# Attention sweep: the order of transposes, scores and value products on TensorE, and of evictions and sigmoids on ScalarE

## What is computed

```python
for nb in range(seq // 128):                      # blocks of 128 queries
    z = einsum('bhtd,bhsd->bhts', qh[t0:t1], kh[:t1]) * scale
    mask = s < t
    log_keep = where(mask, log_sigmoid(-z), 0)
    rc = cumsum(log_keep, axis=keys, reverse=True)
    after = concatenate([rc[..., 1:], 0])
    w = where(mask, exp(log_sigmoid(z) + after), 0)
    out = einsum('bhts,bhsd->bhtd', w, vh[:t1])
```

## Time and profile before

| | us |
|---|---|
| median of 3 runs | 3290.05 |
| lowest and highest | 3288.12, 3293.3 |
| the profiled execution | 3288.1 |
| its span, first to last instruction | 3286.3 |

### The profile page before, as it was taken

How to read it: one execution, slowest core, us unless ns; L and a number is a source line. 1 busy time by engine, 2 the same in 40 slices (tenths; PEclk the granted TensorE clock), 3 DMA queues, 4 the chain that set the end, 5 groups by cost and what they waited for, 6 DMA issues and landing times. The chain is left out here.

```text
span 3286.3 us, 56906 instructions
## 1 busy us (share of the span) xinstructions
PE 3110.6 (95%) x22432; PEld 2724.4 (83%) x22432; DVE 1502.1 (46%) x1651; ACT 975.2 (30%) x1749; POOL 496.8 (15%) x218
## 2 busy tenths in 40 slices
PE   7899999999999999998888859999999999979998
PEld 6788888888999999998888857777777777768887
DVE  4212221111112311122888848778767877654433
ACT  4211111111111111110110126766666767631111
POOL 3211111111011101110664521000000000000000
PEclk8999999999999999999999989999999999989999
DMA  7113444443122221222444336523552351053221
GB/s 277 58 61 97 122 121 121 121 121 115 60 71 70 70 74 58 70 70 111 138 139 145 103 89 144 129 53 78 129 124 58 78 129 40 14 180 121 80 99 38
DMA packets 217944, 327.14 MB, mean 100 GB/s; under 512 B 11680, under 2 KB 159520, under 8 KB 204960
## 3 DMA queue, kind: packets, MB, share of 16 engines
q1 hardware_dynamic: 217296, 324.08, 33.0%
q10 hardware_dynamic: 464, 0.63, 0.1%
HBM read 207.22 MB, written 117.44 MB: 99 GB/s over the span
## 5 line engine op out<-in xcount | busy, mean ns | idle before, releaser
L1092 DVE TENSOR_TENSOR_SCAN run<-akeep 128x768 f32<-128x768 f32 (+7 forms) x256 | 425.5, 1698 | 172.2 <-ACT akeep L1056 122.3
L1064 ACT ACTIVATE wt<-t_ps 128x512 f32<-128x512 f32 (+3 forms) x640 | 314.1, 536 | 129.7 <-PE t_ps L985 128.7
L1056 ACT ACTIVATE akeep<-z_ps 128x1024 f32<-128x1024 f32 (+7 forms) x384 | 291.1, 778 | 155.6 <-PE z_ps L974 144.0
L1006 PE MATMUL o_ps<-wt,ad 128*64 128x128 f32 x4352 | 308.1, 280 | 5.5 <-issue 5.5
L985 PE MATMUL t_ps<-ident,run 128*128 128x128 f32 x2176 | 311.8, 278 | 0.1
L969 PE MATMUL z_ps<-ak,aq 128*128 128x512 f32 (+3 forms) x640 | 253.5, 396 | 40.2 <-DMA aq<-s_qlo 33.7
L370 PE MATMUL u_ps<-w_hi,h_lo 128*128 128x256 f32 x2048 | 287.5, 283 | 0.0
L370 PE MATMUL u_ps<-w_hi,h_hi 128*128 128x256 f32 x2048 | 287.5, 283 | 0.0
L370 PE MATMUL u_ps<-w_lo,h_hi 128*128 128x256 f32 x2048 | 287.5, 283 | 0.0
L1006 PEld LDWEIGHTS o_ps<-wt,ad 128*64 128x64 f32 x4352 | 231.2, 136 | 58.7 <-issue 57.9
L985 PEld LDWEIGHTS t_ps<-ident,run 128*128 128x128 f32 x2176 | 242.3, 141 | 45.1 <-issue 18.7
(11 more groups left out here) (140 smaller groups left out, 3837.7 us busy)
## 6 DMA issues: line engine op xcount, KB each, us to landing
w_raw<-in_w_in SPq DMA_DIRECT2D x32, 1024.0 KB, 5.7
aq<-s_qhi SPq DMA_DIRECT2D x64, 256.0 KB, 6.4
aq<-s_qlo SPq DMA_DIRECT2D x64, 256.0 KB, 7.0
o<-s_o SPq DMA_DIRECT2D x16, 1024.0 KB, 6.3
ada<-in_w_ada SPq DMA_DIRECT2D x9, 1024.0 KB, 7.5
xg<-in_x SPq DMA_DIRECT2D x4, 2048.0 KB, 10.7
s_gq<-st SPq DMA_DIRECT2D x32, 256.0 KB
s_gf<-st SPq DMA_DIRECT2D x32, 256.0 KB
```

Source lines behind the costliest of these rows:

```text
L1006: mm = nc.tensor.matmul(o_ps[e * SD:(e + 1) * SD, cols], delta[:, b, key // P + j, e * SD:(e + 1) * SD], wt[:, a % 8, j * P:(j + 1) * P], ...
L1056: nc.scalar.activation(keepf[:, e, n % 2, 0:width], z_ps[e][:, 0:width], ACT.Sigmoid, scale=-SCALE).then_inc(keep_ready, 1)
L1064: nc.scalar.activation(wt[:, a % 8, 0:wd], t_ps[a % 2][:, 0:wd], ACT.Identity, scale=-1.0, bias=1.0).then_inc(wt_ready, 1)
L1092: nc.vector.tensor_tensor_scan(run[:, e, qb % 2, at0:at0 + width][:, ::-1], keepf[:, e, n % 2, 0:width][:, ::-1], keepf[:, e, n % 2, 0:width],
```

## The change

Nothing is computed differently. The order in a step changes on two engines:
- TensorE: transposes of A (piece n - 2), scores of A and of B (piece n), transposes of B (piece n - 2), then all value products of piece n - 3 in one row. `weighted` loses its chunk argument and waits once, for the eviction of B's last chunk.
- ScalarE: the evictions of A, both sigmoids, the evictions of B.

```diff
-                def weighted(i, n, c):
+                def weighted(i, n):
...
-                    pe.wait_ge(wt_ready, i * (4 * NS) + (lists[1][c][0] + 1))
-                    key, wd = lists[0][c][1:]
-                    for j in range(wd // P):
-                        for e in range(2):
...
+                    pe.wait_ge(wt_ready, i * (4 * NS) + (last_part(n, 1) + 1))
+                    for c in range(len(lists[0])):
+                        key, wd = lists[0][c][1:]
+                        for j in range(wd // P):
+                            for e in range(2):
...
                 def step(i, n, last):
-                    for e in range(2):
-                        if there(n, last):
-                            scores(i, n, e)
-                    for e in range(2):
-                        if there(n - LAG_T, last):
-                            transposes(i, n - LAG_T, e)
-                        if there(n - LAG_AV, last):
-                            weighted(i, n - LAG_AV, e)
+                    if there(n - LAG_T, last):
+                        transposes(i, n - LAG_T, 0)
+                    if there(n, last):
+                        scores(i, n, 0)
+                        scores(i, n, 1)
+                    if there(n - LAG_T, last):
+                        transposes(i, n - LAG_T, 1)
+                    if there(n - LAG_AV, last):
+                        weighted(i, n - LAG_AV)
...
+                    n1 = n - LAG_T
+
+                    def evict(e):
+                        for a, key, wd in part_list(n1, e):
+
+                            act.wait_ge(t_ready, i * (4 * NS) + (a + 1))
+                            nc.scalar.activation(wt[:, a % 8, 0:wd], t_ps[a % 2][:, 0:wd], ACT.Identity, scale=-1.0,
+                                                 bias=1.0).then_inc(wt_ready, 1)
+
+                    if there(n1, last):
+                        evict(0)
                     if there(n, last):
...
-                    n1 = n - LAG_T
                     if there(n1, last):
-                        for e in range(2):
-                            for a, key, wd in part_list(n1, e):
...
+                        evict(1)
```

More of the change, by code:

```diff
@@ L992, in weighted @@
                     lists = [part_list(n, e) for e in range(2)]
-                    if c >= len(lists[0]):
-                        return
-                    if c == 0 and diag and qb % 4 == 0:
+                    if diag and qb % 4 == 0:
                         pe.wait_ge(ot_ready, i * 8 + (4 * (n // NP) + qb // 4 + 1))
-                    if c == 0 and n % NP == 0:
+                    if n % NP == 0:
                         pe.wait_ge(delta_ready, i * 2 + (n // NP + 1))
                     cols = slice((qb % 4) * P, (qb % 4 + 1) * P)
-                    pe.wait_ge(wt_ready, i * (4 * NS) + (lists[1][c][0] + 1))
-                    key, wd = lists[0][c][1:]
-                    for j in range(wd // P):
-                        for e in range(2):
[L1005 to L1010, removed]
+                    pe.wait_ge(wt_ready, i * (4 * NS) + (last_part(n, 1) + 1))
[3 more added lines that the diff above has]
+                            for e in range(2):
+                                a = lists[e][c][0]
+                                mm = nc.tensor.matmul(o_ps[e * SD:(e + 1) * SD, cols], delta[:, b, key // P + j, e * SD:(e + 1) * SD],
+                                                      wt[:, a % 8, j * P:(j + 1) * P], start=(diag and key == lo and j == 0),
+                                                      stop=(lo == 0 and key + (j + 1) * P == width))
+                    mm.then_inc(av_ready, 1)
                 def rows(i, n):
@@ L1057, in step @@
                                                  scale=-SCALE).then_inc(keep_ready, 1)
-                    n1 = n - LAG_T
                     if there(n1, last):
-                        for e in range(2):
-                            for a, key, wd in part_list(n1, e):
-                                act.wait_ge(t_ready, i * (4 * NS) + (a + 1))
-                                nc.scalar.activation(wt[:, a % 8, 0:wd], t_ps[a % 2][:, 0:wd], ACT.Identity, scale=-1.0,
-                                                     bias=1.0).then_inc(wt_ready, 1)
+                        evict(1)
                 sweep(nc.scalar, step)
```

## The result

The changed kernel takes 3241.42 us (median, 3241.3 to 3247.25) against 3289.09 us for the kernel before. The ratio is 0.9859, 95% interval 0.9842 to 0.9876: 1.4% faster. Two more comparisons gave 0.9869 (0.9854 to 0.9884) and 0.9863 (0.9847 to 0.9880), with medians of 3246.39 against 3290.1 and 3242.65 against 3287.79. So the change saves 44 to 48 us where 38.4 were forecast. The direction and the mechanism hold, the size was too small.

The account below looks back on a forecast made before the run. The prediction took TensorE's own row of work as the bound; 42.7 us saved by fewer switches, less 1.3 and 3 of waits, gave 38.4 us, so about 3251.5 us, range 3244 to 3268.

Parts of the forecast that it names:

- The bound: Attention sweep: TensorE is the bound, busy 196.8 of 200 us; only shortening its own row of work can help.
- The price of a change of work: Sweep steps whose value products have two chunks: fewer switches save 0.34 us in 112 steps, 0.29 in 16, together 42.7.
- The 0.29 for the steps with row transposes: In 16 two-chunk steps, row transposes stand between value products and scores; saving taken as 0.29 us each.
- T(A) before narrow scores: Transposes of A ahead of a narrow diagonal score block: 0 to 0.02 us, at most 32 times, taken as 0.
- The tail, 1.3 us: Last three steps: two waits of 0.4 us for A's eviction and 0.5 for the final value products, 1.3 us lost.
- The 0.5 for the last value products: End of the sweep: the final value products wait for B's last eviction, 0.5 us lost.
- ScalarE's margin: Steps with wide scores and one-chunk value products: B's eviction finishes 0.1 to 0.2 us in time, cost taken as 0.
- VectorE's cover at piece 12: Transposes of piece 12 wait 0.6 us for a scan delayed by GpSimd's subtraction, in six pairs; taken as 3 us.
- Sum: Whole kernel: 42.7 - 1.3 - 3 = 38.4 us saved, giving 3249.7 us profiled and a median of about 3251.5.
- The rival of scans met too early in more pieces: Transposes of A also wait for scans in two or three pieces a pair, about 15 us more: 3266; chance 0.17.
- The slower rival: Late scans hold transposes, scores and the next scan; 1.2 us waits in pieces 10 to 15, 3306 us; chance 0.05.
- The rival that no gain is there: TensorE's drain is paid wherever other data starts, or in-order waits replace it: 3290 us; chance 0.06.

Follow-up runs that it names:

- The cut runs: Changed kernel with value products split again: chunk 0 before the transposes of B, chunk 1 behind them; 3304.93 us, ratio 1.0044 to the kernel before.
- run 128*128: Not a follow-up run: in the profile rows of the transposes, the buffer `run` that they read, with its 128*128 shape; no time or ratio of its own.
- the block gone: Changed kernel with GpSimd subtracting only a sixteenth of each values block for the last six pairs of heads; 3243.08 us, ratio 0.9856.
- the block doubled: Changed kernel with GpSimd subtracting each values block twice, one after the other; 3278.78 us, ratio 0.9972.

## Why the prediction was right or wrong

- *The bound.* Right. TensorE's own row, without waits, set the sweep's time, and it does so again after the change.
- *The price of a change of work, 0.34 us for each two-chunk step.* Right in sum. 5.47 us for a pair of heads without a loop turn (109.83 to 104.36 in the traces) over 16 steps is 0.342. The 0.29 for the steps with row transposes was slightly low: 5.34 forecast for a pair, 5.47 measured, 1 us in all. The cut runs settled that the run is what costs, at 0.30 each; the other 0.04 come with the order.
- *T(A) before narrow scores: taken as 0.* Right within 0.06 us: T to Z is 0.03 in the order of starts for widths of 128 and 256, 0.08 for 384.
- *The tail, 1.3 us.* A little too large. The two waits of T(B) for A's eviction came, as 0.34 us of idle engine each; by the starts T(B) follows after 1.43 us instead of 0.87, so each cost 0.56 (0.4 forecast). The 0.5 for the last value products did not come: they stand behind those of the piece before, 64 instructions in a row, and the first 32 give 1.7 us of cover. 1.1 us in all.

```profile
2821.32 1.09 PE L985 MATMUL t_ps<-ident,run 128*128 128x128 f32 x8
2822.75 1.07 PE L985 MATMUL t_ps<-ident,run 128*128 128x128 f32 x8 [0.34 <-ACT wt L1055]
2823.75 3.71 PE L1005 MATMUL o_ps<-wt,ad 128*64 128x128 f32 x64
```

- *ScalarE's margin, taken as 0 cost.* Right. No transposes wait for an eviction in the steady state; the two waits in the waits' view are those of the tail.
- *VectorE's cover at piece 12, taken as 3 us of wait.* This is the term that failed. The new order took what was forecast: in the eighth pair, where no block is near, the cover went from 6.57 us to 3.39, 3.2 less (2.2 + 0.65 + 0.34). The block was to lie 1.7 us later against TensorE and leave the transposes 0.6 us short. The store and the load are as I had them (2637.20 to 2657.24, 20.0 us), and against the start of scan A the subtraction began 1.6 us later (1.42 us ahead of it, 3.04 before). But it took 4.56 us and not 5.53. Before, it had begun at 2687.01 while VectorE was in scans that ran until 2688.2, and had waited for them; the time I read from the row held that wait.

```profile
2685.71 2.46 DVE L1092 TENSOR_TENSOR_SCAN run<-akeep,run 128x512 f32<-128x512 f32 x2
```

Later against VectorE's work, it began at 2657.24 when the scans were at their end (2657.29), and waited for nothing. The 0.97 us so saved turned a wait of 0.6 into a cover of 0.4. (In the second trace of the kernel before it took 4.57 us in this pair too: it began at 2686.18, ahead of a scan that waited for it instead, and the cover was 4.2 us again.) That is the seventh pair. In the second, fourth and sixth the block is likewise 4.6 us, against 5.2 to 5.4 before, and the transposes wait 0.26 us at most. The six pairs were misread as well: in the third and the fifth the block lies 10 to 11 us ahead of piece 12 in the kernel before (2237.37 against scans from 2247.88), and the cover left after the change is 0.4 to 1.7 us. With the block gone the time is the same, with the block doubled each pair loses 3 to 5 us. So the cover was really that thin, and it fell short by 0.1 to 0.4 us in all six pairs together and not by 3. No run moved the block's start alone; that its length made the difference is read from the rows.

- *The rest of the program as it was.* Assumed without a word, and wrong by 1.8 us on the mean of the traces. I carried the single profiled execution's distance to the median (1.95 us) over to the change. The sum's lower end allowed for the waits to stay away, 3248 and 4 us more, but not for that together with a last phase that takes up to 2.9 us less.
- *Sum.* Forecast 42.7 - 1.3 - 3 = 38.4. Measured by the traces: sweep 42.7, or 43.6 at equal clock, and rest 1.8, together 44.5, beside 44 to 48 by the medians. Of the 6 us missed by the traces, 3 are the block, 0.2 the tail, 1 the price of 16 steps, and 1.8 the phases outside. 44.5 us off 3290.05 is 3245.5, inside the range. The further 4 us that took the first median out of it are spread between executions: three of its four were 3241.3 to 3241.5, those of the second comparison 3244.6 to 3246.9, and the fourteen executions of the change on record have a median of 3244.2.
- *The rival of scans met too early in more pieces* (3266) didn't occur. Outside the loop turns the traces of the change show waits for a scan only at piece 12 of the second and the fourth pair.
- *The slower rival* (waits feed themselves) didn't occur. The doubled block shows its beginning: with a wait of about 3 us at piece 12 no second wait for a scan follows in the pair. *The rival that no gain is there* fell: with 127 runs of value products 38 of the 43 us went. The queue rule of the Trainium skill, "TensorE: Matmul & The Clock Gate" (table at the top, engine queue), says that weight loads are pulled ahead of running matmuls; by the gaps of the weight loads, 311 before runs of value products and 191 after, that does not happen where the width changes.

## What to carry to other kernels

A busy TensorE may still lose time at every change between full-width work and 64-column work. Measure a run's cost by the starts of runs of two lengths; what doesn't scale with the length is the price of the switch, and it can be had by ordering alone. When an order is tightened, list for each buffer what cover stands between its last reader and its next writer, and move the other engines' order with it: TensorE's new order alone made the kernel 171 us slower than before. And before a duration of a row is carried to another place, look whether the row waited for something inside it.

## What the runs showed of the hardware

- Entering a run of 64-column value products costs 0.145 us and leaving it 0.155, from or to transposes as well as scores (TensorE's rows of the change and of the cut runs); from transposes to scores the next start comes after 0.03 us (0.08 for a width of 384). "TensorEngine Tiling (Array Packing)" of the Trainium skill (Key Properties) says that a change of tiling mode drains the engine; the traces agree and give the size.
- A scan with its inputs in SBUF and a subtraction on GpSimd exclude each other in both directions: the scans took 6.94 us beside it and 3.94 without, the subtraction 5.53 or 6.16 where it met a scan and 4.56 where it didn't. "SBUF — State Buffer" (Who interferes with whom) has this as an exclusive lock that goes to the first; every row here agrees.
- TensorE's granted clock fell to its lower level, 1.2 GHz, at each loop turn, where TensorE had no matmuls for 2.6 to 3.3 us, and behind the sweep. The time at that level differs between executions of one kernel (17.9 to 22.8 us in the sweep of the change), worth about 2 us. With the block doubled it fell at four of six waits of 2.6 to 3.2 us.
